# Moving the operands of the large matmuls to multiples of 2 KB in SBUF

## The reference

```python
h = swiglu(rms_norm(x, ffn1_pre_g), ffn1_w_gate, ffn1_w_up, ffn1_w_down)   # 2048 -> 5632 -> 2048
x = x + 0.5 * rms_norm(h, ffn1_post_g)
u = rms_norm(x, mix_pre_g)
c_q, c_kv, k_rope, q_m, k_m, v_m = split(u @ w_in)                         # 512, 256, 64, 3 x 1024
a = mla_attention(c_q, c_kv, k_rope, ...)                                  # 8 heads
m = moba_attention(q_m, k_m, v_m)                                          # 8 heads
y = concat([rms_norm(a, mla_out_g), rms_norm(m, moba_out_g)]) @ w_out
x = x + rms_norm(y, mix_post_g)
h = swiglu(rms_norm(x, ffn2_pre_g), ffn2_w_gate, ffn2_w_up, ffn2_w_down)
x = x + 0.5 * rms_norm(h, ffn2_post_g)
```

## Time and profile before

| | us |
|---|---|
| runs of the kernel (three) | 1873.34, 1873.86, 1874.07 (median 1873.86) |
| the profiled execution | 1874.37 |
| its span, from the first to the last instruction | 1872.2 |
| TensorE matmuls busy | 1848.2 |
| VectorE busy | 935.7 |
| ScalarE busy | 799.5 |
| granted TensorE clock, mean share of full speed | 0.997 |

### The profile page before, as it was taken

The page is one execution under the profiler, slowest core; times in us unless marked ns, Lnnn a source line. Parts: engine busy times, 40 slices in busy tenths (PEclk is TensorE's granted clock), DMA queues, the critical chain, the costliest instruction groups (busy, mean ns, idle before and its releaser), DMA issues.

```text
span 1872.2 us, 21514 instructions
## 1 busy us (share of the span) xinstructions
PE 1848.2 (99%) x8233; PEld 1496.8 (80%) x8233; DVE 935.7 (50%) x864; ACT 799.5 (43%) x796; POOL 26.0 (1%) x57
## 2 busy tenths in 40 slices
PE   8999999999999999999999999999999999999998
PEld 6888888888878888788888878888888888788886
DVE  5444444444455555655577564444444444454555
ACT  6333433334444544543347445344333343444443
POOL 0000000000000000000000000000000000000000
PEclk9999999999999999999999999999999999999999
DMA  9545555455555555365442544555555555555553
GB/s 366 180 179 183 189 188 179 179 182 187 182 188 179 189 192 180 132 221 183 177 153 68 180 180 180 180 185 190 185 179 182 183 190 185 179 180 188 194 180 112
DMA packets 49064, 341.11 MB, mean 182 GB/s; under 512 B 5438, under 2 KB 5764, under 8 KB 9092
## 3 DMA queue, kind: packets, MB, share of 16 engines
q1 hardware_dynamic: 48944, 340.58, 50.8%
q10 hardware_dynamic: 84, 0.04, 0.0%
HBM read 338.50 MB, written 2.10 MB: 182 GB/s over the span
## 4 chain that ended last, share of the span: by engine, by line
PE 97%; DVE 1%; ACT 1%; issue 0%; DMA 0%; DVEq 0%; POOL 0%; ACTq 0%
PE banks L1266 25%; PE banks L1171 23%; PE banks L1173 23%; PE banks L1172 23%; PE banks L1236 1%; PE banks L1188 1%; PE banks L1301 0%; PE banks L1429 0%; PE banks L1430 0%; DMA raw<-in_weights 0%; PE banks L1440 0%; ACT w_hi L491 0%; PE banks L1336 0%; DVE w_lo L739 0%; PE banks L1450 0%
## 5 line engine op out<-in xcount | busy, mean ns | idle before, releaser
L739 DVE TENSOR_TENSOR w_lo<-raw,w_hi 128x2048 fp32r<-128x2048 f32 (+3 forms) x229 | 515.2, 2250 | 671.4 <-ACT w_hi L408 671.4
L408 ACT ACTIVATE w_hi<-raw 128x2048 fp32r<-128x2048 f32 (+3 forms) x229 | 431.1, 1882 | 757.2 <-PE banks L1173 752.3
L1171 PE MATMUL banks<-w_hi,act_hi 128*128 128x512 f32 (+1 forms) x1728 | 686.5, 397 | 3.7 <-DVE act_lo L748 2.8
L1173 PE MATMUL banks<-w_hi,act_lo 128*128 128x512 f32 (+1 forms) x1728 | 683.0, 395 | 0.0
L1172 PE MATMUL banks<-w_lo,act_hi 128*128 128x512 f32 (+1 forms) x1728 | 678.8, 393 | 0.0
L1171 PEld LDWEIGHTS banks<-w_hi,act_hi 128*128 128x128 f32 x1728 | 325.5, 188 | 78.4 <-issue 3.9
L1173 PEld LDWEIGHTS banks<-w_hi,act_lo 128*128 128x128 f32 x1728 | 325.1, 188 | 77.7
L1172 PEld LDWEIGHTS banks<-w_lo,act_hi 128*128 128x128 f32 x1728 | 325.6, 188 | 76.8
L1266 PE MATMUL banks<-w_hi,hid_split 128*128 128x512 f32 x1376 | 377.0, 395 | 0.0
L842 DVE TENSOR_TENSOR w_lo<-raw,w_hi 128x2048 fp32r<-128x2048 f32 x87 | 199.4, 2292 | 233.5 <-ACT w_hi L491 233.5
L1266 PEld LDWEIGHTS banks<-w_hi,hid_split 128*128 128x128 f32 x1376 | 258.0, 188 | 63.4 <-DVE hid_split L845 0.5
(11 more groups left out here) (131 smaller groups left out, 638.6 us busy)
## 6 DMA issues: line engine op xcount, KB each, us to landing
raw<-in_weights SPq DMA_DIRECT2D x307, 1024.0 KB, 4.8
raw<-in_weights SPq DMA_DIRECT2D x6, 512.0 KB, 4.0
gain_row<-in_post_gains SPq DMA_DIRECT2D x3, 1024.0 KB, 6.7
raw<-in_weights SPq DMA_DIRECT2D x4, 768.0 KB, 4.2
raw<-in_weights SPq DMA_DIRECT2D x4, 640.0 KB, 3.8
xT<-in_x_turned SPq DMA_DIRECT2D x4, 512.0 KB, 10.4
rows<-in_x SPq DMA_DIRECT2D x2, 1024.0 KB, 13.9
out_rows<-rows SPq DMA_DIRECT2D x8, 256.0 KB, 2.8
```

Of the source, the lines that this page charges most:

```text
L408: nc.scalar.activation(w_hi[:, pc.split, 0:width], raw[:, pc.slot, 0:width], ACT.Copy)\
L739: nc.vector.tensor_tensor(w_lo[:, pc.split, 0:width], raw[:, pc.slot, 0:width], w_hi[:, pc.split, 0:width], ALU.subtract).then_inc(lo_read ...
L1171: nc.tensor.matmul(out_ap, hi, rhs_hi, start=start, stop=False, skip_group_check=chain)
L1173: return nc.tensor.matmul(out_ap, lo, rhs_hi, start=False, stop=stop, skip_group_check=chain)
```

## The change

`rows`, `raw`, `w_hi` and `w_lo` are preceded by a pad of 1,920 bytes, so that with the 128 bytes ahead of it `rows` begins at 18,432 = 9 x 2,048. The large tensors follow one behind the other: `act_hi` and its group directly behind `w_lo` (at 100,352), then `hidT` (133,120), `hid_split` (178,176), `xT` (190,464) and what shares their space, all at multiples of 2,048. `gain_row` and the small tensors move behind them, to 206,848 and up. No tensor changes its size, its type or what it shares space with; no instruction of any engine and no DMA is added, removed or moved.

```diff
+ALIGN_PAD = 1920
...
+        sb("align_pad", [P, ALIGN_PAD // 4])
         rows = sb("rows", [P, TILES, D])
         raw = sb("raw", [P, RAW, PIECE])
         w_hi = sb("w_hi", [P, 2, PIECE], F32R)
         w_lo = sb("w_lo", [P, 2, PIECE], F32R)
+        with ExitStack() as s:
+            act_hi = sb("act_hi", [P, DC, TOKENS], F32R, s)
+            act_lo = sb("act_lo", [P, DC, TOKENS], F32R, s)
+        q2T = sb("q2T", [P, HEADS, TOKENS])
...
+        with ExitStack() as s:
+            hidT = sb("hidT", [P, FC, TOKENS], F32, s)
...
+            hid_split = sb("hid_split", [P, 2, 2, 2, TOKENS], F32R, s)
...
+        with ExitStack() as s:
+            xT = sb("xT", [P, DC, TOKENS], F32, s)
...
+        tab_r = sb("tab_r", [P, TILES, MOBA_TAB])
         gain_row = sb("gain_row", [P, D])
         ident = sb("ident", [P, P])
         mask = sb("mask", [P, 2 * P])
...
         rtotal = sb("rtotal", [P, 2, TILES])
-
-
-        with ExitStack() as s:
-            act_hi = sb("act_hi", [P, DC, TOKENS], F32R, s)
-            act_lo = sb("act_lo", [P, DC, TOKENS], F32R, s)
...
```

## The result

The changed kernel takes 1827.76 us (median of 4 runs, 1827.19 to 1828.28) against 1873.6 us for the kernel before (4 runs, 1873.17 to 1874.07): a ratio of 0.9755, 95% interval 0.9743 to 0.9767. I had forecast no change. The profiled execution took 1827.7 us, of which 1825.5 are span: 46.7 us less than the 1872.2 before.

A forecast was written before the change was run, and what follows sets the result against it. TensorE's matmul pace was taken to bound the kernel. All parts of the change summed to 0, so the median of the kernel before, 1873.9 us, was forecast again, with a range of 1871.4 to 1876.4 us.

The forecast's parts named there:

- What bounds the kernel: TensorE's matmul pace: each 512-wide matmul takes 0.2334 us, 20 ns above a column per cycle; other engines barely count.
- the width argument under the moving operands: w_hi, w_lo: from 512 and 320 columns, a start costs at most 2.5 ns a matmul, bounding the gain at 19 us.
- The test on the 320-wide slices: Moving slices crossing a 2 KB boundary and clear ones both took 0.88 us per six matmuls; crossing taken as 0.
- The stationary operands: act_hi, act_lo, hid_split: one in four weight slices crosses 2 KB, but loads are covered by the matmul; taken as 0.
- Elementwise work, small tensors and DMA: ScalarE and VectorE work, small tensors, raw and xT landings: taken as 0, within 1.1 us and 0.1 us either way.
- A: Rival: layout sets TensorE's rate per column; slope falls to a column per cycle, gaining 132 us, to 1742 us; 4%.
- B: Rival: the fixed part of each matmul goes, whole or in part, down to 1855 us; 3%.
- C: Rival: weight and moving slices starting on equal offsets delay each fourth slice's load, 162 us slower, 2036 us; 4%.

The follow-up runs named there:

- e3: Changed kernel without its pad, so weights and activations all start 128 bytes past a multiple of 2 KB: 1827.52 us.
- e4: Changed kernel with its pad 32 bytes longer, so weights and activations all start 32 bytes past a multiple of 2 KB: 1827.35 us.
- e8: Kernel before with one edit, 96 unused bytes ahead of act_hi, weights left where they were: 1827.18 us, ratio 0.9751.
- e1: Changed kernel with all tensors from act_hi on 32 bytes further, weights still on a multiple of 2 KB: 1872.71 us, ratio 0.9994.
- e12: Changed kernel, four alternating matmuls replacing three per product; w_lo and act_hi 96 bytes past a multiple of 256, w_hi and act_lo on one: 2269.67 us.
- e13: Changed kernel, four alternating matmuls replacing three per product; w_lo and act_lo 96 bytes past a multiple of 256, w_hi and act_hi on one: 2295.30 us.
- e7: Changed kernel with pads setting weight-to-stationary distances of 224 and 320 bytes in gate/up, 352 and 448 in the down-projection: 1862.53 us.
- e9: Changed kernel with 16 bytes between the two weight slots' starts and hid_split 32 bytes further (distances 0, 16, 224, 240): 1854.34 us.
- e11: Changed kernel with 24 bytes between the two weight slots' starts and hid_split shifted (distances 0, 24, 224, 248): 1865.47 us.
- e2: Changed kernel with weights moved to 128 bytes past a multiple of 2 KB, act_hi and what follows on a multiple: 1867.82 us, ratio 0.9968.

## Why the prediction was wrong

**What bounds the kernel** was right: TensorE's pace, 233.3 ns against 213.3 ns of columns, and the question where the 20 ns come from was the right one.

**The step that failed** is the width argument under the moving operands: "A price of the crossing, or of any misplaced first or last line, is paid once per slice and cannot depend on the slice's width." For a crossing it held: in e3 and e4 every 2 KB weight slice crosses a 2 KB boundary, and they run as fast as the changed kernel. But the price that was there was of another kind. It belongs to the pair of operands, and at the distance of before, 96 bytes, it does depend on the width: 6.7 ns at 512 columns, 3 at 384, 0 at 320. I drew a line through two widths and called its height at zero, 2.5 ns, the most that a start can cost. Without the price the three widths lie on another line, a column per cycle plus 13.3 ns (213.3 + 13.3 = 226.7; 160 + 13.3 = 173.3; 133.3 + 13.3 = 146.7). The 0.034 ns by which my slope of 0.451 lies over a column per cycle were the price, mixed in. Two points cannot tell that. The third was in the trace: my line gave 175.7 ns for 384 columns, where the rows of before have 176.5. That gap is small, but it was there to be asked about.

**The test on the 320-wide slices** was read rightly, and a crossing is free. But it told nothing of this price, since at 96 bytes this width carries none of it. That crossing and clear slices were alike there was extended to 512 columns, where the trace of before held no contrast.

**The stationary operands** were costed at 0 on the ground that crossing slices kept 0.70 us a triple. True, and beside the point: all slices of `act_hi` lie at one distance from the weights modulo 256 bytes, so those triples held no contrast. In e8 the move of the stationary tensors by 96 bytes, with the weights where they were, brought the whole gain (1827.18 us).

**Elementwise work, small tensors and DMA** were right: VectorE's group at L739 has a mean of 2250 ns on both pages, and the busy times of VectorE and ScalarE agree within 0.4 us. The first landing took 4.04 us instead of 4.25, within the bounds given. It is not the alignment of `raw`: in e1, where `raw` lies as in the changed kernel, it took 4.30 us, and in e8, where it lies as before, 4.30 as well.

**The rivals.** A (the rate per column, 1742 us) fell; the gain is a third of it. B (something per matmul goes) has the right sign, but its bound of 2.5 ns was the failed step again: 6.7 ns came at 512 columns, and its mark, both widths shorter by the same, did not. C had the pair that e12 and e13 bear out in part, stream and weight load, and the wrong sign. I held equal starts for the dangerous case. My evidence against it, that a 512-wide read passes over all offsets while the next weights load, showed only that they overlap; the kernel before was already paying. Had I asked what the trace would look like if it were paying all along, I would have seen that nothing in it spoke against that, and a gain by the same mechanism would have had a chance of its own.

The Trainium skill (SBUF — State Buffer, Who interferes with whom) says that PE and ACT never wait on anyone. The Trainium skill (TensorE: Matmul & The Clock Gate, Step-by-step: what each phase is for) says that loading the next weights does not take read bandwidth from the running matmul. By these sentences the place of the two tensors should not matter. The measurements differ: with the same instructions on the same data, 96 bytes between two tensors are worth 2.5% of the kernel (e8). Where inside the chip the time goes, no run shows.

## What to carry to other kernels

When a stream of matmuls with a weight load each is the bound, compare the distance between starts with columns / 2.4 GHz at several widths; an excess that changes from width to width is not a fixed cost. Then look at the starts of the moving and the stationary tensors modulo 256 bytes and make them equal; here that took one pad of 96 bytes, and multiples of 2 KB gave nothing more. Measure it at your own width: 0 was the best distance tried at 512 columns, not at 320. A steady pace is no proof of a free one: a cost that every instruction pays leaves no contrast in one trace.

## What the runs showed of the hardware that was not expected

- The pace of float32r matmuls of 128 x 128 by 512, each with its weight load, depends on the distance of the two operands' starts modulo 256 bytes: 226.7 ns at 0, 228.9 at 64, 231.7 to 236.7 at the other ten tried. It is not fixed by it in all cases: at 320 bytes, 8 of 106 pieces ran at 233.3 ns and the rest at 228.9 (e7).
- At distance 0 the pace is 213.3 + 13.3, 160 + 13.3 and 133.3 + 13.3 ns at 512, 384 and 320 columns. At distance 96 it is 6.7, 3 and 0 ns more. At other distances 320 columns take 145.2 ns (16 bytes, e9) or 148.7 (24 bytes, e11), and 384 columns 180.0 (496 bytes, e9). Why the widths differ was not tried.
- The pace settles over some seven to ten matmuls after a turn (42 turns of the changed kernel). Where the distance is not 0, single distances between starts of 512 columns spread around a steady mean (227 to 242 ns in e2), so a few starts are not enough to read the pace.
